# A two-layer mixer kernel: the layer change in two token halves, and the recurrence's short convolution one block ahead

## The chip, the core and the metric

The kernel runs on one core of a Trainium2 chip. The metric is the device time of one execution in microseconds (us). A core has a matrix engine (PE; its weight loads are listed apart as PEld), a vector engine (DVE), a scalar engine (ACT), GpSimd (POOL) and a queue that issues DMAs (SP). Each engine runs its own instructions in order; between engines there are only semaphores.

## What is computed

Two layers over 256 latent and 256 context tokens of width 2048, float32. A layer normalises and modulates its input, multiplies it with one wide matrix, runs three branches on the columns (a convolution module, a recurrence in both directions, attention), gates them, and multiplies with an output matrix:

```
def mixer_layer(x, xc, ...):
    h, gate = modulate(x, norm_g, (c_act @ w_ada + b_ada)[:, None, :])
    hc, gate_c = modulate(xc, norm_g, cc_act @ w_ada + b_ada)
    u = h @ w_in
    uc = hc @ (w_in[:, :OFF_MEM_END] if last else w_in)
    ...
    x = x + gate * (jnp.concatenate([y_conv, y_lru, y_attn], axis=-1) @ w_out)
    if not last:
        xc = xc + gate_c * (jnp.concatenate([yc_conv, yc_lru, yc_attn], axis=-1) @ w_out)

def modulate(x, norm_g, ada):                       # rmsnorm is x * rsqrt(mean(x*x) + EPS) * g
    shift, scale, gate = jnp.split(ada, 3, axis=-1)
    return rmsnorm(x, norm_g) * (1 + scale) + shift, gate

def rglru_scan(x, h0, conv_w, conv_b, w_r, b_r, w_i, b_i, lam):
    xc = depthwise_conv(x, conv_w, conv_b, (LRU_CONV_WIDTH - 1, 0))      # four taps
    r = sigmoid(blocks(xc) @ w_r + b_r);  i = sigmoid(blocks(xc) @ w_i + b_i)
    log_a = -LRU_C * r * softplus(-lam);  a = exp(log_a)
    bx = sqrt(-expm1(2 * log_a)) * (i * xc)
    # h[t] = a[t] * h[t-1] + bx[t], by an associative scan
```

## The kernel before

**Layout and blocks.** Activations lie transposed: the partition is the channel, the free axis the token (0 to 255 latent, 256 to 511 context). `Y` [128, 16, 512] holds the stream, and in layer 1 the context half of its rows is free for the branches. A layer is `NB` = 56 blocks of 128 output columns: 4 recurrence inputs `x`, keys and values `k`, `v`, the convolution's `b` and `a` (in layer 1 these eight come first: b4 is `b0`, b5 `a0`, up to b11 `a3`; then `k0`, `k1`, `v0`, `v1` as b12 to b15), queries, gates, and from `B_OUT` = 40 on 16 output blocks. In the text bN is block N of a layer.

**Products.** A float32 matrix is split in a high part, rounded by ACT (`hi`, L962), and a rest, from DVE (`lo`, L1261); activations too (`h_hi`, `h_lo`). A block is 16 tiles deep, three products each (hi by hi, hi by lo, lo by hi; L756 to L758), so 48 products, made in two halves of 24 (`mm_half`). There are four buffers of half a block of weights (a unit `u` uses `u % 4`), so `hi` of a unit waits for the products of the unit four before. A product has 512 columns where all tokens are needed, 256 in layer 1's latent-only blocks. Every engine's program walks over the same blocks; in block b ACT and DVE prepare the weights of block b + 2, then take the result of block b out of PSUM (`evac`), then do the side work that tables such as `LRU_TAPS`, `LRU_MM` and `CONV_TAPS` assign to the block.

**Layer change.** Output block b54 and b55 end layer 0. DVE adds each output block, times its gate, to the residual (L1398), ACT squares it (L991), DVE adds the squares up (L1306). PE sums over partitions with a matrix of ones (`rms_mm`, L670 and L672), ACT takes the root (L998), DVE the reciprocal (`rstd`, L1339). Then DVE modulates tile k (L1326), ACT rounds it (L1004), DVE makes the rest (L1333). In that time PE makes `gate_sum` (L623) and `bridge(4)`, 32 products whose result nobody reads (L631). Layer 1 opens with four blocks side by side in four PSUM banks: `mm_first_quarter` does tiles 0 to 3 for all four (48 products, L712 to L714), then `mm_quarter` the rest, two blocks at a time.

**Recurrence.** Four groups t of 128 channels, two directions d. `taps` (DVE, L1428 and L1432, 8 instructions) is the four-tap convolution, into `T[:, 4 * d]`; `lru_mm` (PE, L780) four float32 products that read it; `lru_act` (ACT, L1048 to L1063) two gates and their powers; `lru_v` (DVE, L1438, L1440); `lru_sqrt` (ACT); `lru_scan` (DVE, L1447 to L1461), which ends in the same `T[:, 0]` and `T[:, 4]`. So `taps` of group t + 1 must wait for the scan of group t. In the tables a list is for layer 0, one for layer 1, and the entries are the blocks of t = 0 to 3; within a block DVE runs `lru_v`, `lru_scan` and `taps` after the evacuation.

## Time and profile before

| | us |
|---|---|
| median of 3 runs (1279.43 to 1281.43) | 1280.09 |
| the profiled execution's own time | 1280.23 |
| span of its trace | 1278.4 |
| PE busy | 1229.1 |
| DVE busy | 794.5 |
| ACT busy | 542.5 |

The profiled execution lies 0.14 us from the median, and 1.83 us of its time are outside the span. Times in the text are us from the start of the span. Idle time of an engine counts only where the chain that ended last goes through it.

### The profile page before, as it was taken

How to read it: one execution, taken by the hardware profiler on the slowest of the kernel's cores; microseconds unless marked ns; L12 is line 12 of the kernel's file. 1: busy time of each engine (PE TensorE's matmuls, PEld its weight loads, DVE VectorE, ACT ScalarE, POOL GpSimd, SP SyncE). 2: the span in 40 equal slices, each digit the busy share in tenths (PEclk: the TensorE clock that was granted, in tenths of full speed). 3: DMA queues.
4: the chain of work that ended last, by engine and by line, in shares of the span. 5: the costliest groups of instructions: out<-in, count | busy, mean ns of one | idle time of the engine just before them, and what ended most of it. 6: DMA issues, size and time to landing. Idle time of an engine off the chain costs nothing.

```text
span 1278.4 us, 16662 instructions
## 1 busy us (share of the span) xinstructions
PE 1229.1 (96%) x6722; PEld 972.0 (76%) x6722; DVE 794.5 (62%) x1249; ACT 542.5 (42%) x853; POOL 9.8 (1%) x11
## 2 busy tenths in 40 slices
PE   3999999999999999999999999999999999999995
PEld 1555776667677777776778888788787988889995
DVE  5344446687566676663466555695689977646554
ACT  5222444452233434453342222354656455475442
POOL 0000100000000000000100000000000000000000
PEclk9999999999999999999999999999999999999998
DMA  9999755446663343332438666413332544325542
GB/s 334 350 348 348 233 211 202 198 198 259 251 246 147 139 176 132 132 132 99 177 137 280 222 222 222 173 66 132 132 104 70 200 144 151 122 87 197 189 165 66
DMA packets 80877, 236.34 MB, mean 185 GB/s; under 512 B 9376, under 2 KB 54176, under 8 KB 59424
## 3 DMA queue, kind: packets, MB, share of 16 engines
q1 hardware_dynamic: 80800, 235.27, 52.0%
q8 instruction: 53, 0.87, 0.3%
q14 instruction: 24, 0.20, 0.0%
HBM read 230.54 MB, written 2.10 MB: 182 GB/s over the span
## 4 chain that ended last, share of the span: by engine, by line
PE 88%; DVE 4%; ACT 3%; SPq 3%; issue 1%; DMA 1%; DVEq 0%; ACTq 0%
PE psum_block L756 21%; PE psum_block L757 21%; PE psum_block L758 21%; PE psum_ada L614 3%; PE psum_scores L780 2%; SPq L563 2%; PE psum_ada L651 2%; PE psum_scores L692 1%; PE psum_scores L817 1%; PE psum_scores L694 1%; PE psum_scores L693 1%; PE psum_scores L850 1%; PE psum_scores L830 1%; DVE T L1432 1%; PE psum_block L877 1%
## 5 line engine op out<-in xcount | busy, mean ns | idle before, releaser
L756 PE MATMUL psum_block<-h_hi,w_hi 128*128 128x512 f32 (+1 forms) x1616 | 556.0, 344 | 2.3 <-DVE h_lo L1253 1.7
L757 PE MATMUL psum_block<-h_lo,w_hi 128*128 128x512 f32 (+1 forms) x1616 | 547.7, 339 | 0.0
L758 PE MATMUL psum_block<-h_hi,w_lo 128*128 128x512 f32 (+1 forms) x1616 | 547.6, 339 | 0.0
L1261 DVE TENSOR_TENSOR w_lo<-raw,w_hi 128x1024 fp32r<-128x1024 f32 x210 | 254.3, 1223 | 312.2 <-ACT w_hi L962 312.0
L962 ACT ACTIVATE w_hi<-raw 128x1024 fp32r<-128x1024 f32 x210 | 221.1, 1058 | 486.6 <-PE psum_block L758 454.0
L756 PEld LDWEIGHTS psum_block<-h_hi,w_hi 128*128 128x128 f32 x1616 | 306.4, 190 | 65.3 <-issue 26.5
L757 PEld LDWEIGHTS psum_block<-h_lo,w_hi 128*128 128x128 f32 x1616 | 306.6, 190 | 33.8 <-issue 1.9
L758 PEld LDWEIGHTS psum_block<-h_hi,w_lo 128*128 128x128 f32 x1616 | 306.5, 190 | 33.8
L1474 DVE SCALAR_TENSOR_TENSOR Y<-glu,small,Y 128x512 f32<-128x512 f32 (+1 forms) x240 | 130.4, 611 | 0.0
L1077 ACT ACTIVATE T<-psum_scores,stats 128x512 f32<-128x512 f32 (+1 forms) x48 | 28.9, 616 | 46.5 <-DVE stats L1522 46.5
L614 PE MATMUL psum_ada<-raw,cstat 128*32 128x512 f32 x384 | 47.8, 600 | 0.0
L1004 ACT ACTIVATE h_hi<-T,ada 128x256 fp32r<-128x256 f32 x64 | 27.8, 499 | 43.2 <-DVE T L1326 43.2
L1261 DVE TENSOR_TENSOR w_lo<-qreg,w_hi 128x1024 fp32r<-128x1024 f32 (+1 forms) x16 | 17.5, 1092 | 30.3 <-ACT w_hi L962 29.2
L780 PE MATMUL psum_scores<-T,bd 128*128 128x512 f32 x64 | 30.8, 626 | 5.5 <-DVE T L1432 5.5
L1295 DVE SCALAR_TENSOR_TENSOR kv<-raw,cstat,kv 128x2048 f32<-128x2048 f32 x15 | 35.2, 2343 | 0.2
L1438 DVE SCALAR_TENSOR_TENSOR qreg<-qreg,T 128x512 f32<-128x512 f32 x16 | 10.3, 687 | 37.8 <-ACT qreg L1063 37.8
L1083 ACT ACTIVATE T<-T,stats 128x512 f32<-128x512 f32 (+1 forms) x48 | 27.3, 641 | 13.6 <-DVE stats L1532 13.6
L1432 DVE SCALAR_TENSOR_TENSOR T<-qreg,small,T 128x512 f32<-128x512 f32 x48 | 32.5, 745 | 0.0
L991 ACT ACTIVATE T<-Y 128x512 f32<-128x512 f32 (+1 forms) x48 | 25.7, 548 | 16.0 <-DVE Y L1398 13.3
L962 ACT ACTIVATE w_hi<-qreg 128x1024 fp32r<-128x1024 f32 (+1 forms) x16 | 15.1, 945 | 30.7 <-DMA qreg<-in_w_blocks 30.7
L1306 DVE TENSOR_TENSOR T<-T 128x512 f32<-128x512 f32 (+1 forms) x43 | 25.7, 599 | 3.2 <-ACT T L991 1.8
L692 PE MATMUL psum_scores<-h_hi,w_hi 128*128 128x512 f32 x64 | 27.7, 433 | 0.0
(200 smaller groups left out, 1183.5 us busy)
## 6 DMA issues: line engine op xcount, KB each, us to landing
raw<-in_w_blocks SPq DMA_DIRECT2D x105, 1024.0 KB, 4.9
raw<-in_w_ada SPq DMA_DIRECT2D x81, 1024.0 KB, 6.8
qreg<-in_w_blocks SPq DMA_DIRECT2D x8, 896.0 KB, 11.6
glu<-in_w_ada SPq DMA_DIRECT2D x5, 1024.0 KB, 11.9
...
```

The lines of the kernel that those rows point to most:

```text
L614: last = mm(psA[32 * j:32 * j + 32, :], cstat[:, c_at(k):c_at(k) + 32], w[:, j * TOK:(j + 1) * TOK], start=(k == 0), stop=(k == DT - 1), t ...
L692: mm(ps, hi, hh[:, k, :], start=(k == 0), stop=False)
L756: mm(ps[:, 0:n], hi, hh[:, k, t], start=(at == 0), stop=False)
L757: mm(ps[:, 0:n], hi, hl[:, k, t], start=False, stop=False)
L758: last = mm(ps[:, 0:n], lo, hh[:, k, t], start=False, stop=(at == DT - 1))
L780: last = mm(psS[:, 2 * d + g, :], bd[:, g, d * CT + t, :], T[:, 4 * d, :], start=True, stop=True)
L962: fn(wh[:, u % 4, 0:cols.stop - cols.start], raw_of(item)[:, cols], ACT.Copy).then_inc(*C.up("hi", u))
L1077: fn(T[:, g, k0:TOK], psS[:, g, k0:TOK], ACT.Exp, scale=SCALE, bias=st[:, 1, g:g + 1], accum_out=st[:, 2, g:g + 1]).then_inc(*C.up("att_ex ...
L1261: V.tensor_tensor(wl[:, u % 4, 0:n], raw_of(item)[:, cols], wh[:, u % 4, 0:n].bitcast(F32), ALU.subtract).then_inc(*C.up("lo", u))
L1295: stt(acc, w, cstat[:, c_at(k):c_at(k) + 1], acc, ALU.mult, ALU.add).then_inc(*C.up("gate_acc", k))
L1432: stt(out, x, lcw[:, c, k:k + 1], out, ALU.mult, ALU.add).then_inc(*C.up("taps", l, t, d))
L1474: stt(out, x, dwh[:, c:c + 1], out, ALU.mult, ALU.add).then_inc(*C.up("conv", l, t, k))
```

## The change

1. **Output blocks by token half.** Blocks b54 and b55 of layer 0 are made in the order: latent columns of b54, latent of b55, then context of b54, context of b55 (eight pieces of 24 products with 256 columns). The four weight buffers are held until the context pieces. `evac_half` takes each half out by itself.
2. **Two norm chains.** Squares, sum, root, reciprocal, modulation and rests are made by token half (`norm_in_halves` on ACT and DVE, `rms_mm_half` on PE). The sum over partitions of the latent half stands between the pieces of the context half; that of the context half after the first tile of the first quarter.
3. **First quarter in halves.** `mm_first_quarter` does tiles 0 to 3 with the latent columns, then with the context columns. `rms_mm(1)` and `bridge(4)` are gone, `gate_sum` stays.
4. **Recurrence.** `taps` writes to `lru_x(t, d)`, rows 8 to 15 of `Y` in the context columns, two sets in turn. It stands a block or two earlier for t = 1 to 3. `lru_mm` of layer 1 is at b6, b9, b11, b13 (it was b6, b9, b12, b14). `lru_v` goes with `lru_sqrt` (`LRU_ROOT`), the scan one block behind it, and both are now ahead of the second `lo` of a block on DVE. `lru_act(t)` waits for the scan of t - 1. Eight entries of layer 1's `CONV_TAPS` differ, with the same sum.

Line numbers in the rows of after are those of the changed kernel.

```diff
-BRIDGE = [14, 4, 6, 8, 32]
-
-
-LRU_TAPS = [[7, 9, 11, 13], [4, 7, 10, 13]]
-LRU_MM = [[8, 10, 12, 14], [6, 9, 12, 14]]
-LRU_SCAN = [[9, 11, 13, 15], [7, 10, 13, 15]]
+BRIDGE = [14, 4, 6, 8]
+SPLIT_FROM = NB - 2
+
+
+LRU_TAPS = [[7, 8, 10, 12], [4, 6, 9, 11]]
+LRU_MM = [[8, 10, 12, 14], [6, 9, 11, 13]]
+LRU_ROOT = [[9, 11, 13, 15], [7, 10, 12, 14]]
+LRU_SCAN = [[10, 12, 14, 16], [8, 11, 13, 15]]
 CONV_AT = [12, 8]
 CONV_TAPS = [[4, 3, 2, 3, 3, 4, 3, 3, 3, 3, 4, 3, 3, 3, 3, 3, 3, 3, 3, 3],
-             [3, 0, 2, 3, 3, 8, 6, 3, 1, 2, 3, 2, 1, 3, 2, 4, 4, 1, 2, 3, 3, 3]]
+             [1, 1, 2, 0, 6, 7, 6, 5, 1, 2, 3, 2, 1, 3, 2, 4, 4, 1, 2, 3, 3, 3]]
...
+        def lru_x(t, d):
+
+            m = 8 + 4 * (t % 2) + 2 * d
+            return Y[:, m:m + 2, LAT:TOK]
...
                     pe.wait_ge(*C.at("lo", quarter_unit(0, pair)))
                 for b in range(2):
                     pe.wait_ge(*released(NB + b - 2))
-                pe.wait_ge(*C.at("rms_std", 1))
-                for i in range(QT):
-                    pe.wait_ge(*C.at("h_lo", 1, i))
-                    for pair in range(SIDE // 2):
-                        quarter_products(0, pair, i)
+                for s in range(2):
+                    for i in range(QT):
+                        pe.wait_ge(*C.at("h_lo", 1, i, s))
+                        for pair in range(SIDE // 2):
+                            quarter_products(0, pair, i, tokens(s))
+                        if s == 0 and i == 0:
+                            rms_mm_half(1)
 
             def mm_quarter(quarter, pair):
 
                 pe.wait_ge(*C.at("lo", quarter_unit(quarter, pair)))
                 for i in range(QT):
                     if pair == 0:
...
                 for i in range(DT // 2):
                     at = j * DT // 2 + i
                     k = k_tile(b, at)
                     if b == B_OUT:
                         pe.wait_ge(*C.at("y_lo", l, k))
                     hi, lo = wh[:, slot, i * P:(i + 1) * P], wl[:, slot, i * P:(i + 1) * P]
-                    mm(ps[:, 0:n], hi, hh[:, k, t], start=(at == 0), stop=False)
-                    mm(ps[:, 0:n], hi, hl[:, k, t], start=False, stop=False)
-                    last = mm(ps[:, 0:n], lo, hh[:, k, t], start=False, stop=(at == DT - 1))
-                last.then_inc(*C.up("mm", u))
+                    mm(ps[:, cols], hi, hh[:, k, t], start=(at == 0), stop=False)
+                    mm(ps[:, cols], hi, hl[:, k, t], start=False, stop=False)
+                    last = mm(ps[:, cols], lo, hh[:, k, t], start=False, stop=(at == DT - 1))
+                if s != 0:
+                    last.then_inc(*C.up("mm", u))
+                elif j:
+                    last.then_inc(*C.up("mm_lat", gb))
 
             def misc_free(l):
...
@@ -901,9 +935,7 @@
                 if b == 0:
                     scores_free.clear()
                     if l:
-                        rms_mm(l)
                         gate_sum()
-                        bridge(4)
                         mm_first_quarter()
                         for quarter in range(1, 4):
                             for pair in range(SIDE // 2):
...
                         for g in range(GROUPS):
                             mm_group(g)
                 if b < OPEN[l]:
+                    continue
+                if in_halves(gb):
+                    mm_half(gb, 0, 0)
+                    mm_half(gb, 1, 0)
+                    if b == NB - 1:
+                        mm_half(gb - 1, 0, 1)
+                        rms_mm_half(0)
+                        mm_half(gb - 1, 1, 1)
+                        mm_half(gb, 0, 1)
+                        mm_half(gb, 1, 1)
                     continue
                 mm_half(gb, 0)
 
...
+            def norm_in_halves():
+
+
+                square_half(DT - 2, 0)
+                square_half(DT - 1, 0)
+                hi(quarter_unit(0, 0))
+                rms_std_half(0)
+                hi(quarter_unit(0, 1))
+                square_half(DT - 2, 1)
+                modulate_list([(k, 0) for k in range(QT)])
+                hi(quarter_unit(1, 0))
+                square_half(DT - 1, 1)
+                hi(quarter_unit(1, 1))
+                modulate_list([(QT, 0)])
+                rms_std_half(1)
+                modulate_list([(k, 1) for k in range(QT + 1)] + [(k, i) for k in range(QT + 1, 2 * QT) for i in range(2)])
 
             def evac(gb):
                 l, b = divmod(gb, NB)
...
@@ -1043,6 +1122,8 @@
             def lru_act(l, t):
 
                 act.wait_ge(*C.at("lru_mm", l, t))
+                if t:
+                    act.wait_ge(*C.at("lru_h", l, t - 1))
...
+                dve.wait_ge(*C.at("rms_add", 1, m - 1))
+                V.tensor_tensor(T[:, 4, w], T[:, 4, w], T[:, squares(1)[m % 2], w], ALU.add).then_inc(*C.up("rms_add", 1, m, s))
+
+            def rstd_half(s):
+                dve.wait_ge(*C.at("rms_std", 1, s))
+                V.reciprocal(tbuf[:, tokens(s)], tbuf[:, tokens(s)]).then_inc(*C.up("rstd", 1, s))
+                dve.wait_ge(*C.ago("rstd"))
+
+            def norm_in_halves():
+
+
+                rms_add_half(DT - 2, 0)
+                evac_half(NB - 1, 0)
+                lo(quarter_unit(0, 0))
+                rstd_half(0)
+                evac_half(NB - 2, 1)
+                h_list([(k, 0) for k in range(QT)])
+                lo(quarter_unit(0, 1))
+                rms_add_half(DT - 2, 1)
+                evac_half(NB - 1, 1)
+                lo(quarter_unit(1, 0))
+                h_list([(QT, 0)])
+                rstd_half(1)
+                h_list([(k, 1) for k in range(QT)])
+                lo(quarter_unit(1, 1))
+                h_list([(QT, 1)] + [(k, i) for k in range(QT + 1, 2 * QT) for i in range(2)])
 
             def rstd(l):
                 n = TOK if l < LAYERS else LAT
...
+            def evac_half(gb, s):
+
+                i, w = gb - B_OUT, tokens(s)
+                dve.wait_ge(*(C.at("mm", unit(0, gb, 1)) if s else C.at("mm_lat", gb)))
+                if s == 0:
+                    dve.wait_ge(*C.at(f"xs{i % 2}", i))
+                stt(Y[:, i, w], bank(gb)[:, w], ada[:, 0, s, GATE * DT + i:GATE * DT + i + 1], T[:, i % 2, w], ALU.mult, ALU.add
+                    ).then_inc(*(C.up("evac_dve", gb) if s else C.up("evac_lat", gb)))
 
             def evac(gb):
                 l, b = divmod(gb, NB)
...
                 dve.wait_ge(*C.at("evac_act", l * NB + t))
-                if t:
-                    dve.wait_ge(*C.ago("lru_h"))
+                if t > 1:
+                    dve.wait_ge(*C.at("lru_g", l, t - 2, 1))
                 for k in range(LTAPS):
                     for d in range(2):
                         c = (l * 2 + d) * CT + t
                         s = k if d == 0 else 2 * (LTAPS - 1) - k
                         x = lrux[:, t, :, s:s + LAT]
-                        out = segs(T[:, 4 * d, :])
+                        out = lru_x(t, d)
                         if k == 0:
                             V.tensor_scalar(out, x, lcw[:, c, 0:1], at["lcb"][:, c:c + 1], ALU.mult, ALU.add
...
                     continue
                 if b == B_OUT:
                     y_lo(l, b)
-                if gb + 2 < GLOB:
+                if gb == NB - 1:
+                    norm_in_halves()
+                    continue
+                if gb + 2 < GLOB and not in_halves(gb):
                     lo(unit(0, gb + 2, 0))
+                if b in LRU_ROOT[l]:
+                    lru_v(l, LRU_ROOT[l].index(b))
+                if b in LRU_SCAN[l]:
+                    lru_scan(l, LRU_SCAN[l].index(b))
                 if l == 0 and b == B_OUT - 1:
                     y_lo(l, b)
```

PE at the layer change, from the last output products to the first of layer 1. Before: the sum over partitions (`psum_scores<-T`), the gate's sum (`psum_ada<-kv`), the bridge (`psum_scores<-rounded`), then the first quarter:

```order
L758 MATMUL psum_block<-h_hi,w_lo 128x512
L670 MATMUL psum_scores<-T,small 128x512
L672 MATMUL psum_scores<-T,small 128x512
L623 MATMUL psum_ada<-kv,small 32x512 x4
L631 MATMUL psum_scores<-rounded 128x384 x32
L712 MATMUL psum_block<-h_hi,w_hi 128x512
```

After:

```order
L787 MATMUL psum_block<-h_hi,w_hi 128x256
L788 MATMUL psum_block<-h_lo,w_hi 128x256
L789 MATMUL psum_block<-h_hi,w_lo 128x256
L636 MATMUL psum_ada<-kv,small 32x512 x4
L735 MATMUL psum_block<-h_hi,w_hi 128x256
L736 MATMUL psum_block<-h_lo,w_hi 128x256
```

The gate's sum now stands directly between the last output product and the first of layer 1, and the latent half's sum over partitions stands 72 products ahead of it. The context half's sum is inside the first quarter.

DVE at the layer change. Before: last evacuation of b55 (L1398), last squares, rest of the fourth unit of weights, reciprocal, then the tiles of layer 1:

```order
L1398 SCALAR_TENSOR_TENSOR Y<-psum_block,ada,T 128x256 x2
L1306 TENSOR_TENSOR T<-T 128x512
L1261 TENSOR_TENSOR w_lo<-raw,w_hi 128x1024
L1339 RECIPROCAL tbuf<-tbuf 128x512
L1326 SCALAR_TENSOR_TENSOR T<-Y,A,tbuf 128x256 x4
```

After, from the latent evacuation of b55 to its context evacuation:

```order
L1496 SCALAR_TENSOR_TENSOR Y<-psum_block,ada,T 128x256
L1340 TENSOR_TENSOR w_lo<-raw,w_hi 128x1024
L1442 RECIPROCAL tbuf<-tbuf 128x256
L1496 SCALAR_TENSOR_TENSOR Y<-psum_block,ada,T 128x256
L1404 SCALAR_TENSOR_TENSOR T<-Y,A,tbuf 128x256 x2
L1410 SCALAR_TENSOR_TENSOR h_lo<-T,ada,h_hi 128x256
L1404 SCALAR_TENSOR_TENSOR T<-Y,A,tbuf 128x256
L1410 SCALAR_TENSOR_TENSOR h_lo<-T,ada,h_hi 128x256
L1404 SCALAR_TENSOR_TENSOR T<-Y,A,tbuf 128x256
L1410 SCALAR_TENSOR_TENSOR h_lo<-T,ada,h_hi 128x256 x2
L1340 TENSOR_TENSOR w_lo<-raw,w_hi 128x1024
L1438 TENSOR_TENSOR T<-T 128x256
```

The evacuation of b55's context half (the next L1496) is behind four latent tiles and a rest of weights.

DVE in layer 1, from b6 on. Before: rests for b8, then `lru_v(0)`, rests for b9, the scan of t = 0, `taps(1)`:

```order
L1261 TENSOR_TENSOR w_lo<-raw,w_hi 128x1024 x2
L1438 SCALAR_TENSOR_TENSOR qreg<-qreg,T 128x512 x2
L1440 SCALAR_TENSOR_TENSOR T<-T 128x512 x2
L1261 TENSOR_TENSOR w_lo<-raw,w_hi 128x1024 x2
L1374 SCALAR_TENSOR_TENSOR glu<-tbuf,psum_block 128x256
L1447 TENSOR_TENSOR T<-T,qreg 128x512 x2
L1451 SCALAR_TENSOR_TENSOR T<-T 128x256
L1454 SCALAR_TENSOR_TENSOR T<-T 128x512
L1457 SCALAR_TENSOR_TENSOR T<-T 128x256
L1461 TENSOR_TENSOR Y<-T 128x256
L1428 TENSOR_SCALAR T<-qreg,small 128x512 x2
L1432 SCALAR_TENSOR_TENSOR T<-qreg,small,T 128x512 x6
```

After (L1562 and L1566 are `taps`, L1572 and L1575 `lru_v`, L1582 the first of the scan):

```order
L1340 TENSOR_TENSOR w_lo<-raw,w_hi 128x1024 x2
L1562 TENSOR_SCALAR Y<-qreg,small 128x2x256 x2
L1566 SCALAR_TENSOR_TENSOR Y<-qreg,small,Y 128x2x256 x6
L1340 TENSOR_TENSOR w_lo<-raw,w_hi 128x1024
L1572 SCALAR_TENSOR_TENSOR qreg<-qreg,T 128x512 x2
L1575 SCALAR_TENSOR_TENSOR T<-T,Y 128x512 x2
L1340 TENSOR_TENSOR w_lo<-raw,w_hi 128x1024
L1508 SCALAR_TENSOR_TENSOR glu<-tbuf,psum_block 128x256
L1340 TENSOR_TENSOR w_lo<-raw,w_hi 128x1024
L1582 TENSOR_TENSOR T<-T,qreg 128x512 x2
```

`taps(1)` moved from behind the scan of t = 0 to ahead of `lru_v(0)`, and `lru_v` and the scan to between the two rests of a block.

## Rows read from the trace of the kernel before

**Rows 1.** The page: the chain that ended last, by engine.

```profile
PE 88%; DVE 4%; ACT 3%; SPq 3%; issue 1%; DMA 1%; DVEq 0%; ACTq 0%
```

**Rows 2.** PE's waits: waiting line, releaser: us in total, times, longest.

```profile
PE psum_scores L780 <- DVE T L1432: 5.5, 3, 2.8
```

**Rows 3.** PE in order of time, layer change: start, us, line, operation, count, [idle before].

```profile
798.57 0.39 PE L756 MATMUL psum_block<-h_hi,w_hi 128*128 128x512 f32 x1
...
820.11 0.39 PE L758 MATMUL psum_block<-h_hi,w_lo 128*128 128x512 f32 x1
822.06 1.13 PE L670 MATMUL psum_scores<-T,small 128*128 128x512 f32 x2 [1.57 <-DVE T L1306]
...
823.98 1.07 PE L623 MATMUL psum_ada<-kv,small 128*32 128x512 f32 x8
824.97 5.82 PE L631 MATMUL psum_scores<-rounded 128*128 128x384 f32 x32
831.05 0.47 PE L712 MATMUL psum_block<-h_hi,w_hi 128*128 128x512 f32 x1 [0.26 <-DVE h_lo L1333]
...
842.03 0.39 PE L712 MATMUL psum_block<-h_hi,w_hi 128*128 128x512 f32 x1
```

**Rows 4.** PE in order of time, b5 of layer 1.

```profile
883.74 0.28 PE L756 MATMUL psum_block<-h_hi,w_hi 128*128 128x256 f32 x1
883.86 0.28 PE L757 MATMUL psum_block<-h_lo,w_hi 128*128 128x256 f32 x1
```

**Rows 5.** PE in order of time, final norm: a sum over partitions with 256 columns.

```profile
1265.11 0.70 PE L670 MATMUL psum_scores<-T,small 128*128 128x256 f32 x2 [0.91 <-DVE T L1306]
1265.65 0.59 PE L672 MATMUL psum_scores<-T,small 128*128 128x256 f32 x2
```

**Rows 6.** ACT in order of time, layer change.

```profile
809.71 1.06 ACT L962 ACTIVATE w_hi<-raw 128x1024 fp32r<-128x1024 f32 x1 [4.38 <-PE psum_block L758]
...
823.04 1.28 ACT L998 ACT_TABLE_LOAD   x1
```

**Rows 7.** DVE in order of time: layer change, then a reciprocal of the final norm.

```profile
812.73 2.34 DVE L1295 SCALAR_TENSOR_TENSOR kv<-raw,cstat,kv 128x2048 f32<-128x2048 f32 x1
...
830.94 0.88 DVE L1326 SCALAR_TENSOR_TENSOR T<-Y,A,tbuf 128x256 f32<-128x256 f32 x2
...
832.65 0.88 DVE L1326 SCALAR_TENSOR_TENSOR T<-Y,A,tbuf 128x256 f32<-128x256 f32 x2
...
1267.39 1.75 DVE L1339 RECIPROCAL tbuf<-tbuf 128x256 f32<-128x256 f32 x1 [2.33 <-ACT tbuf L998]
```

**Rows 8.** Groups of DVE instructions from 760 to 880: count | busy, mean ns.

```profile
L1261 DVE TENSOR_TENSOR w_lo<-raw,w_hi 128x1024 fp32r<-128x1024 f32 x21 | 25.7, 1225 | 39.8 <-ACT w_hi L962 39.6
```

**Rows 9.** SP's queue in order of time, layer change.

```profile
801.18 0.33 SPq L563 DMA_DIRECT2D raw<-in_w_ada  x1
...
804.65 0.50 SPq L504 DMA_DIRECT2D T<-in_xT  x1
```

**Rows 10.** DMAs of line L563, 790 to 850: from issue to landing.

```profile
DMA to landing us min/median/max: 4.6/4.9/6.1
```

**Rows 11.** PE in order of time: four of the recurrence's eight product groups.

```profile
208.83 3.70 PE L780 MATMUL psum_scores<-T,bd 128*128 128x512 f32 x8 [0.66 <-DVE T L1432]
...
916.05 5.40 PE L780 MATMUL psum_scores<-T,bd 128*128 128x512 f32 x8 [2.80 <-DVE T L1432]
...
943.70 3.60 PE L780 MATMUL psum_scores<-T,bd 128*128 128x512 f32 x8
...
971.08 3.70 PE L780 MATMUL psum_scores<-T,bd 128*128 128x512 f32 x8 [2.00 <-DVE T L1432]
```

**Rows 12.** DVE in order of time, layer 1: scan of t = 0, then `taps(1)`.

```profile
906.81 1.28 DVE L1447 TENSOR_TENSOR T<-T,qreg 128x512 f32<-128x512 f32 x2
...
911.93 4.06 DVE L1432 SCALAR_TENSOR_TENSOR T<-qreg,small,T 128x512 f32<-128x512 f32 x6
```

**Rows 13.** Stretches: us, busy time and count of each engine, granted clock, DMA.

```profile
900.00:920.00 20.00, 17.20 (x117) 14.68 (x116) 18.07 (x28) 12.40 (x15) 0.00 (x0) 0.91 0.18 58
```

135 lines of the change are left out of this document (89 added, 46 removed).

## The prediction

> **What bounds the kernel.** I read the page's chain first: PE holds 88% of it [rows 1], so only time in which PE stands still, or makes something that the result doesn't need, can be won. PE's waits come next: after the start of the program the largest is that of the recurrence's products, 5.5 us in three pieces [rows 2]. Then PE in order of time. At the layer change the last output product starts at 820.11. PE stands still 1.57 us until the squares are summed, makes the sum over partitions (822.06 to 823.98, that is 1.92), the gate's sum (0.99) and then the bridge (824.97 to 831.05, 6.08 with the wait behind it), whose result nobody reads [rows 3]. It covers the chain root, reciprocal, modulation. In all 10.7 us lie between the end of layer 0's products (820.34) and the first of layer 1 (831.05), and 2.9 of them are needed work. The rest of the change touches the recurrence: of eight groups of products, five show no idle time before them and three do, 0.66, 2.80 and 2.00 us, each released by the last of `taps` [rows 11].
>
> **Part 1: output blocks in halves.** 96 products with 512 columns become 192 with 256. The two blocks now take 798.57 to 820.34, 226.8 ns a product [rows 3]. Layer 1's products with 256 columns start 120 ns apart [rows 4]. A pair costs 13.2 ns more than a whole; 96 pairs make 1.27 us, the first quarter's 48 make 0.63. The cost is 1.9 us, all of it on PE's path. The same weights, operands and banks are behind both rows, so I take it as it is.
>
> The row shows 120 ns for 256 columns and 227 for 512. The Trainium skill, page "TensorE: Matmul & The Clock Gate", section "Back-to-back issue gap", gives N / 2.4 + 2.5 ns at the full clock, that is 109 and 216: by it a pair costs 2.5 ns more, 0.4 us in all, and the sum below would be 1.5 us lower. The rows differ from it and they decide.
>
> **Part 2: PE's new calendar at the change.** Eight pieces of 24 products take 2.88 us each. From 798.57: latent half of b54 ready at 804.3, of b55 at 810.1; first context piece of b54 to 812.97; the latent sum over partitions, by the final norm's two lines 0.54 + some 0.43, so 0.97 [rows 5]; second piece of b54 to 816.8, b55 to 819.7 and 822.6; the gate's sum 0.99 to 823.6. From there on PE could begin layer 1.
>
> Is the latent sum ready? `evac_half` of b54 at 804.8, the gate's accumulation 2.34 [rows 7], whose weights are issued at 801.18 and land 4.9 later, at 806.1 [rows 9, 10], squares and adds by 809.3. The residual of b55, issued at 804.65 [rows 9], takes about as long and lands at 809.6, ahead of 810.1. `evac_half` of b55, then the square, are done at 811.1: 1.9 us early. The two moved DMAs have no later start than before, since SP waits for the accumulation of gate rows 14, which doesn't move.
>
> **Part 3: the chain on DVE and ACT.** ACT rounds unit 1 of layer 1 when the first context piece is done (0.25 after it, as the row at 809.71 stands to its product), 813.2 to 814.3, loads the root's table (1.28) [rows 6], and makes the root of 256 columns by 816.1, since the sum is there at 814.2. DVE: rest of the unit (1.23) [rows 8] to 815.5; reciprocal of 256 columns 1.75 [rows 7] to 817.85; context evacuation of b54 to 818.3. A tile with both halves takes DVE 830.94 to 832.65, 1.71 [rows 7], so a half tile 0.86; four latent half tiles with 0.3 to fill the pipe end at 822.05. Behind them on DVE are the rest of unit 2 (to 823.25), an add of squares (0.4) and the context evacuation of b55 (0.45), at 824.1. `mm_first_quarter` waits for both, the unit and `released`, which is this evacuation; queued behind it on PE is all of layer 1. So **layer 1 starts at 824.15**, 0.55 us after PE is free.
>
> Latent part of the quarter: 48 products, 5.76, with the context sum (0.97) after the first 12, which ends at 826.6. To 830.9. The context chain from 826.6: root 0.45 (the table is loaded), reciprocal 1.75 to 829.05, two modulations, first rest at 830.3, then 0.86 for each further tile. PE wants them at 830.9, 832.3, 833.8 and 835.2: no wait, with 0.6 us in hand at the first. Context part to 836.65. The second quarter wants tiles 4 to 7 at 836.65 and then every 1.36. DVE makes a rest of weights to 833.8 and seven half tiles at 0.86, to 840.1, and PE wants the last at 840.7. Later quarters have over 1 us in hand. Before, the second quarter began at 842.03 [rows 3]. **Won: 842.03 − 836.65 = 5.4 us**, the 1.9 of part 1 already in it. The bridge's and the first idle time's 7.7 go, 1.9 come, 0.55 are the new wait; the rest is rounding.
>
> **Part 4: recurrence.** The three waits for `taps` are 0.66 (layer 0) and 2.80 + 2.00 (layer 1). Behind the one of 2.80 the group took 5.40 us against 3.60 for one without [rows 11], and the granted clock of 900 to 920 is 0.91 [rows 13]: after that idle time a part of the work ran at 1.2 GHz instead of 2.4. Together 0.66 + 2.80 + 2.00 + 1.80 = 7.3 us.
>
> Do the waits go? From 906.81 to 915.99 DVE makes the scan and then `taps(1)` [rows 12], while PE stands still from 913.25. After, `taps(1)` follows the rests for b8, is done by 900 in the old calendar and is wanted at 913.25. `taps(2)` is wanted at 913.25 + 3.5 + 11.5 = 928.3. DVE's work from 904.5 (first rest for b9) to its end: `lru_v` 2.4, five rests 6.0, two evacuations 0.8, scan 4.1, convolution 0.7, taps 5.0, 19.0 us, so 923.5. `taps(3)` is wanted 25 us later still, with 16 us of work ahead of it. The second rest of each block now stands behind `lru_v` or a scan: that of b10 is done at 915.1 and wanted at 919.6, that of b11 at 918.2 and wanted at 925.3. ACT's group t waits for the scan of t − 1: for t = 2 this is at 936.3 instead of 931.7, and the first unit behind it on ACT, for b14, is wanted 14 us after. In layer 0 blocks take twice as long and all of this has more in hand. `taps` has the same instructions, now written in two segments of 256, and `lru_mm` reads them so. No row shows that. The six of L1432 already read two segments and take 4.06 [rows 12]; I take 0 for both, with half a us either way in the range.
>
> **Sum.** 5.4 + 7.3 = 12.7 us. The profiled execution took 1280.23; less 12.7 is 1267.5. It stands 0.14 above the median, so against the median of 1280.09 I say **1267.4**. Not on a changed path are the start of the program and everything from b17 of layer 1 on, which moves as a whole.
>
> **Rivals.**
> A, the new queue on DVE decides at the layer change. The context evacuation of b55 stands behind ten instructions and four handoffs to ACT, and the context chain has only 0.6 in hand. If each handoff costs 0.3 more, the start slips by 1.2 and the context tiles by as much; two us are lost, and with an idle time near the 2.80 that cost clock in [rows 11, 13] another 1.8. For it: DVE's busy time from 813 on is without a gap in my calendar. Against it: the half tile's 0.86 has the handoffs of two halves in it. Time 1267.4 + 2 to 3.8 = 1269.4 to 1271.2.
> B, the recurrence doesn't deliver: its waits come back as waits for rests of weights in b10 to b12, because `lru_v` and the scan (6.5 us) now stand ahead of them. It begins when DVE is more than 4.5 us behind my calendar at b10. Then half of the 7.3 is lost: 1271.0.
> C, slower than before: without the bridge the clock falls. PE makes 0.97 of small work and has 0.55 idle at 823, and if that brought the granted clock to its lower level, products would take twice as long. To eat 12.7 us it has to last for more than 12.7 us of PE's work, from the change to past the middle of the second quarter; over both quarters (22.9 us of work) it is + 22.9, so 1290. Against it: 1.57 idle at 820 is followed by no slow product, and the dip behind 2.80 idle cost 1.8 only [rows 3, 11].
> The same page of the Trainium skill, section "What's actually happening", says that the clock's default is the lower level and activity lifts it, which would put C's start where the array has little to do; the trace agrees with that direction at 916, and not at 822.
> D, the change doesn't do what it says at one place, as when the half sums wait for each other: PE waits in the first quarter for the context chain by several us, and 5.4 becomes 2. 1270.8.
>
> **Chances.** Forecast 0.68, A 0.16, B 0.06, D 0.05, C 0.03, more gain than forecast 0.02. The forecast's own range: without the new wait it is 0.55 lower, and the slower first products behind each idle time may save 0.8 more; the calendar's rounding may cost 1.4. So from 1266.0 to 1268.8. A, B and D reach to 1271.2. The range for 8 in 10 goes from 1265.8 to 1271.0. A measurement of this kernel tells 0.2% (2.6 us) from no change; all but C and a stray case lie below 1277.5: faster 0.95, same 0.02, slower 0.03.
>
> **What would show it.** Right: the idle time before the first quarter in PE's order of time is under 1 us; the second quarter starts 5.4 us earlier than 842.03; the only idle time of PE in the quarters is there; no wait of the recurrence's products for `taps`; each of the eight groups 3.6 to 3.7 us long; the stretch of 20 us about b9 at a granted clock of 1.00. Wrong: a wait of PE for the evacuation or a rest at the change over 1.5 us (A), waits for the rests of weights about b10 (B), a granted clock under 1 from 823 on (C), waits for `h_lo` inside the quarters (D). Products of 256 columns more than 120 ns apart would move part 1.

## The result, and the profile of the changed kernel

| | before | after |
|---|---|---|
| median of 4 runs, us | 1280.76 (1279.43 to 1281.45) | 1269.27 (1268.70 to 1270.52) |
| the profiled execution | 1280.23 | 1269.71 |
| span of its trace | 1278.4 | 1267.9 |

The ratio is 0.9904, with a 95% interval from 0.9887 to 0.9922. The changed kernel is 11.5 us faster by the medians and 10.5 by the profiled executions. I had said 1267.4 (12.7 us won), in a range of 1265.8 to 1271.0.

To see where the time went, I set the start of the same product in both traces side by side, at the places where one stage gives way to the next:

| first product of | before | after | gained since the row above |
|---|---|---|---|
| b7 of layer 0 | 153.89 | 155.07 | −1.19 |
| b54 of layer 0 | 798.57 | 798.97 | +0.80 |
| b4 of layer 1 | 874.67 | 869.95 | +5.12 |
| b9 of layer 1 | 907.33 | 903.79 | −1.20 |
| b10 of layer 1 | 920.88 | 912.64 | +4.71 |
| b17 of layer 1 | 992.07 | 981.54 | +2.29 |
| last product | 1263.92 | 1253.40 | 0.00 |

Each gain is the difference of the two columns, less what the rows above it had already gained. Two rows are negative, and neither was in my sum. The rest adds up to 12.9, against 12.7 in the sum.

PE's waits in the trace of after (columns: waiting group, what released it, us in total, times, longest):

```profile
PE psum_scores L680 <- DVE T L1385: 20.0, 1, 20.0
...
PE psum_block L787 <- DVE glu L1508: 1.0, 1, 1.0
...
PE psum_block L735 <- DVE Y L1496: 0.9, 1, 0.9
```

The entry that was second to the opening's in [rows 2], 5.5 us for `taps`, is gone: no wait of the recurrence's products (now L814) is left. Two are new. L735 is the first quarter's product, held by the context evacuation of b55 (L1496). L787 is a product of b9, held by an evacuation (L1508).

The layer change on PE in order of time, trace of after (start, duration, form, count, and the idle time ahead with its releaser):

```profile
813.36 0.59 PE L692 MATMUL psum_scores<-T,small 128*128 128x256 f32 x2
...
822.72 0.28 PE L789 MATMUL psum_block<-h_hi,w_lo 128*128 128x256 f32 x1
822.93 1.06 PE L636 MATMUL psum_ada<-kv,small 128*32 128x512 f32 x8
824.85 0.36 PE L735 MATMUL psum_block<-h_hi,w_hi 128*128 128x256 f32 x1 [0.85 <-DVE Y L1496]
...
837.28 0.40 PE L735 MATMUL psum_block<-h_hi,w_hi 128*128 128x512 f32 x1
```

Against [rows 3]: 2.0 us instead of 10.7 lie between the end of layer 0's products (822.84, one spacing of 0.12 behind the start of the last) and layer 1's first (824.85). The latent sum (813.36) runs without a wait between the context pieces, and the second quarter starts at 837.28 instead of 842.03.

The same place on DVE, trace of after, with the context evacuation of b55 at 824.12 and what stands ahead of it:

```profile
816.50 1.75 DVE L1442 RECIPROCAL tbuf<-tbuf 128x256 f32<-128x256 f32 x1 [0.56 <-ACT tbuf L1047]
818.29 0.48 DVE L1496 SCALAR_TENSOR_TENSOR Y<-psum_block,ada,T 128x256 f32<-128x256 f32 x1
...
822.65 1.22 DVE L1340 TENSOR_TENSOR w_lo<-raw,w_hi 128x1024 fp32r<-128x1024 f32 x1
823.78 0.42 DVE L1438 TENSOR_TENSOR T<-T 128x256 f32<-128x256 f32 x1
824.12 0.48 DVE L1496 SCALAR_TENSOR_TENSOR Y<-psum_block,ada,T 128x256 f32<-128x256 f32 x1
...
830.78 0.49 DVE L1410 SCALAR_TENSOR_TENSOR h_lo<-T,ada,h_hi 128x256 fp32r<-128x256 f32 x1 [0.18 <-ACT h_hi L1055]
```

The new loss stands ahead of b9. On PE, and on DVE in the 6 us before it, trace of after:

```profile
902.48 0.28 PE L789 MATMUL psum_block<-h_hi,w_lo 128*128 128x256 f32 x1
903.79 0.36 PE L787 MATMUL psum_block<-h_hi,w_hi 128*128 128x256 f32 x1 [1.04 <-DVE glu L1508]
```
```profile
898.55 1.23 DVE L1340 TENSOR_TENSOR w_lo<-raw,w_hi 128x1024 fp32r<-128x1024 f32 x1 [3.43 <-ACT w_hi L1004]
899.69 1.28 DVE L1572 SCALAR_TENSOR_TENSOR qreg<-qreg,T 128x512 f32<-128x512 f32 x2
900.89 1.29 DVE L1575 SCALAR_TENSOR_TENSOR T<-T,Y 128x512 f32<-128x512 f32 x2
902.10 1.22 DVE L1340 TENSOR_TENSOR w_lo<-raw,w_hi 128x1024 fp32r<-128x1024 f32 x1
903.23 0.41 DVE L1508 SCALAR_TENSOR_TENSOR glu<-tbuf,psum_block 128x256 f32<-128x256 f32 x1
```

PE could begin b9 at 902.6, but its PSUM bank is that of b7, and b7's result is taken out at 903.23. Two rests of weights and the four instructions of `lru_v` (L1572, L1575) are queued ahead of that. Ahead of the first rest DVE stood idle for 3.43 us.

The recurrence's products (shortest, median and longest in ns), and two stretches with their granted clock (PEclk), trace of after:

```profile
L814 PE MATMUL psum_scores<-Y,bd x64: 590/592/595, 179.8 to 952.8; 128*128 128x512 f32 x64
```
```profile
core 0: us, PE busy (x) PEld busy (x) DVE busy (x) ACT busy (x) POOL busy (x), PEclk, DMA share, GB/s
820.00:835.00 15.00, 14.14 (x116) 13.03 (x114) 12.95 (x23) 6.38 (x12) 0.00 (x0) 1.00 0.40 141
892.00:912.00 20.00, 18.96 (x144) 17.54 (x143) 16.30 (x24) 15.59 (x20) 0.00 (x0) 1.00 0.29 103
```

Not one of the 64 products lasts over 595 ns, and the clock is at its upper level about the change and about b9, where [rows 13] had 0.91.

### The profile page after: what moved, and what is told of

Its sections match the earlier page's. It is cut to its first block, busy times and chain, and to the rows that moved or that the text cites. A ratio compares the mean times of both kernels' runs of the same rounds, so it can differ in the third digit from the quotient of the medians.

```text
span 1267.9 us, 16907 instructions
## 1 busy us (share of the span) xinstructions
PE 1223.3 (96%) x6838; PEld 975.4 (77%) x6838; DVE 796.6 (63%) x1251; ACT 544.3 (43%) x856; POOL 9.7 (1%) x11
## 4 chain that ended last, share of the span: by engine, by line
PE 91%; ACT 3%; DVE 2%; SPq 2%; DMA 1%; issue 1%; DVEq 0%; ACTq 0%
PE psum_block L787 22%; PE psum_block L788 21%; PE psum_block L789 21%; PE psum_ada L627 4%; PE psum_ada L664 2%; PE psum_scores L814 2%; PE psum_scores L715 1%; SPq L576 1%; PE psum_scores L717 1%; PE psum_scores L716 1%; PE psum_scores L851 1%; PE psum_scores L884 1%; PE psum_scores L864 1%; DMA bd<-in_w_ada 1%; PE psum_block L911 1%; PE psum_misc L911 1%
## 5 line engine op out<-in xcount | busy, mean ns | idle before, releaser
L787 PE MATMUL psum_block<-h_hi,w_hi 128*128 128x256 f32 (+1 forms) x1648 | 561.9, 341 | 3.4 <-DVE h_lo L1332 1.7
L788 PE MATMUL psum_block<-h_lo,w_hi 128*128 128x256 f32 (+1 forms) x1648 | 553.4, 336 | 0.0
L789 PE MATMUL psum_block<-h_hi,w_lo 128*128 128x256 f32 (+1 forms) x1648 | 553.2, 336 | 0.0
L787 PEld LDWEIGHTS psum_block<-h_hi,w_hi 128*128 128x128 f32 x1648 | 312.6, 190 | 65.2 <-issue 28.2
L788 PEld LDWEIGHTS psum_block<-h_lo,w_hi 128*128 128x128 f32 x1648 | 312.9, 190 | 32.8 <-issue 1.9
L789 PEld LDWEIGHTS psum_block<-h_hi,w_lo 128*128 128x128 f32 x1648 | 312.8, 190 | 32.7
L1566 DVE SCALAR_TENSOR_TENSOR Y<-qreg,small,Y 128x512 f32<-128x512 f32 x48 | 32.5, 748 | 0.0
L1033 ACT ACTIVATE T<-Y 128x512 f32<-128x512 f32 (+1 forms) x46 | 24.5, 546 | 12.9 <-DVE Y L1532 10.1
L1410 DVE SCALAR_TENSOR_TENSOR h_lo<-T,ada,h_hi 128x256 fp32r<-128x256 f32 x64 | 27.9, 481 | 1.7 <-ACT h_hi L1055 1.7
L814 PE MATMUL psum_scores<-Y,bd 128*128 128x512 f32 x64 | 28.8, 592 | 0.0
L1404 DVE SCALAR_TENSOR_TENSOR T<-Y,A,tbuf 128x256 f32<-128x256 f32 x64 | 27.7, 481 | 0.6
## 6 DMA issues: line engine op xcount, KB each, us to landing
qreg<-in_w_blocks SPq DMA_DIRECT2D x8, 896.0 KB, 11.7
```

The source lines that it names most:

```text
L787: mm(ps[:, cols], hi, hh[:, k, t], start=(at == 0), stop=False)
L788: mm(ps[:, cols], hi, hl[:, k, t], start=False, stop=False)
L789: last = mm(ps[:, cols], lo, hh[:, k, t], start=False, stop=(at == DT - 1))
L814: last = mm(psS[:, 2 * d + g, :], bd[:, g, d * CT + t, :], lru_x(t, d), start=True, stop=True)
L1566: stt(out, x, lcw[:, c, k:k + 1], out, ALU.mult, ALU.add).then_inc(*C.up("taps", l, t, d))
```

## The experiments

Each experiment was timed in several runs beside the kernel before on the same chip; kernels timed together share those runs. Two traces are compared from the first product of b7 of layer 0 on where the openings differ.

### The same program again, and the two parts alone

**after_again** is the changed kernel once more. 

> The changed kernel once more, unchanged, beside the kernels that take it apart. Two theories of the 1.2 us that it had lost by b7 of layer 0, where it has the same instructions as before: by the first it is the spread of the opening's DMAs, and the first product of b7 starts anywhere from 153.9 (before) to 155.1 (after) in each kernel, whatever it holds; by the second it belongs to the changed program, and b7 starts at 155.1 here too and in each kernel that has the halves. All else as in the trace of after: second quarter about 4.9 us earlier than before counted from b7, a wait of 1.0 us of PE ahead of b9 of layer 1. Ratio to before 0.989 to 0.992.

Measured: 1269.43 us (1268.25 to 1270.45) against 1281.72 (1278.42 to 1284.22), ratio 0.9898 [0.9885, 0.9912]. In its trace b7 starts at 153.89, exactly as before, and from there every place of the table above is 1.2 us earlier than in the first trace of after. The instructions are the same. What differs lies ahead of 60 us: the lengths of the waits for the first DMAs, and the granted clock, which from 36 to 44 is 0.57 in the first trace of after, 0.79 here and 1.00 in before. So the row −1.19 is not the change's. Against this trace the span of before is 11.73 us longer.

**halves_only** keeps parts 1 to 3 and takes part 4 back:

```diff
-LRU_TAPS = [[7, 8, 10, 12], [4, 6, 9, 11]]
-LRU_MM = [[8, 10, 12, 14], [6, 9, 11, 13]]
-LRU_ROOT = [[9, 11, 13, 15], [7, 10, 12, 14]]
-LRU_SCAN = [[10, 12, 14, 16], [8, 11, 13, 15]]
+LRU_TAPS = [[7, 9, 11, 13], [4, 7, 10, 13]]
+LRU_MM = [[8, 10, 12, 14], [6, 9, 12, 14]]
+LRU_SCAN = [[9, 11, 13, 15], [7, 10, 13, 15]]
+LRU_ROOT = LRU_SCAN
...
-            m = 8 + 4 * (t % 2) + 2 * d
-            return Y[:, m:m + 2, LAT:TOK]
+            return segs(T[:, 4 * d, :])
```

> The layer change in halves with the recurrence as it was. Additive theory: it gains at the layer change what the traces of before and after show there, 5.1 us (5.4 forecast), nothing elsewhere: the three waits for the taps are back (0.7, 2.8, 2.0) with the slow group behind the one of 2.8, and there is no wait ahead of b9. Time 1275.4 for a before of 1280.5, ratio 0.996. Rival, that the layer change's gain is lost when DVE comes out of it with less in hand: PE waits more for taps in layer 1, gain 3 us or less.

Measured: 1277.38 us, ratio 0.9958 [0.9946, 0.9970], span 1273.4, 5.09 less than before. The waits for `taps` are back, and with them the group at the lower clock:

```profile
PE psum_scores L813 <- DVE T L1563: 5.5, 3, 2.8
```
```profile
911.01 1.22 PE L813 MATMUL psum_scores<-T,bd 128*128 128x512 f32 x1 [2.81 <-DVE T L1563]
```

Its b9 starts 5.76 us after b8 (896.52, 902.28), that is without the new wait.

**recurrence_only** is before with part 4 alone, the same lines in the other direction. 

> The recurrence's edits with the layer change as it was. Additive theory: 0.8 us in layer 0 and 5.8 in layer 1, in which the new wait of 1.2 ahead of b9 (for the evacuation of a1, b7, now behind lru_v on DVE) is already taken off: 6.6 us, time 1273.9, ratio 0.995; this wait stands here too. Rival: the wait ahead of b9 comes from the earlier layer change, with DVE still behind from it; then it isn't here, and the gain is 7.8 us, ratio 0.994.

Measured: 1273.67 us, ratio 0.9936 [0.9924, 0.9948], span 1271.8, 6.64 less than before. The wait ahead of b9 is in it, of the same size:

```profile
PE psum_block L762 <- DVE glu L1382: 1.0, 1, 1.0
```

5.09 and 6.64 make 11.73, the whole of `after_again`. The medians confirm the sum, and split it otherwise: against the 1281.72 of before in these runs 4.34 and 8.05 are won, 12.39 together, and 12.29 by `after_again`. The traced execution of `halves_only` (1275.14) is the fastest of its five, and the 17 of before go from 1278.42 to 1284.22, so each share is known no better than to a microsecond or so. The parts don't touch each other, and the new wait belongs to part 4. The layer change doesn't cause it.

### Where `lru_v` and the scan stand

**side_work_behind** is the changed kernel with `lru_v` and the scan back behind the evacuation, in their new blocks (the four lines stood ahead of the block's second `lo`, and now follow `evac`):

```diff
-                if b in LRU_ROOT[l]:
-                    lru_v(l, LRU_ROOT[l].index(b))
-                if b in LRU_SCAN[l]:
-                    lru_scan(l, LRU_SCAN[l].index(b))
...
+                if b in LRU_ROOT[l]:
+                    lru_v(l, LRU_ROOT[l].index(b))
+                if b in LRU_SCAN[l]:
+                    lru_scan(l, LRU_SCAN[l].index(b))
```

> The changed kernel with lru_v and the scan back behind the evacuation on DVE; taps stay early and in their own buffers. If the gain in the recurrence comes from taps alone, ahead and in two buffers, all of it stays (no wait of a recurrence product for taps), and the wait ahead of b9 goes: 1.2 us faster than the changed kernel. Rival, that lru_v and the scan had to be earlier: ACT's next group then waits for the scan, its rounding of weights comes late, and PE waits for w_lo or evacuations about b10 to b14: slower than the changed kernel by 1 us or more.

Measured: 1282.74 us (11 runs), ratio 1.0008 [0.9998, 1.0019], span 1280.8, which is 14.1 over `after_again`. The wait ahead of b9 is gone (905.74 to 911.50, 5.76 us), so that much of the theory holds, and far more is lost elsewhere. In layer 0 alone it is 9.6 us, nearly all of it in two places. At the first, ACT and then PE in the trace of `side_work_behind`:

```profile
274.30 0.69 ACT L1129 ACTIVATE T<-psum_scores,small 128x512 f32<-128x512 f32 x1 [3.73 <-DVE Y L1596]
```
```profile
281.10 0.66 PE L650 MATMUL psum_ada<-rounded,lnr 128*128 128x128 f32 x4 [2.60 <-ACT lnr L1014]
```

`lru_act` waits for the scan of the group before (part 4 put this wait in), 3.73 us here and none for the scan in `after_again`. ACT's copy out of `psum_ada` (L1014) is queued behind `lru_act`, and PE waits 2.60 us for it. At the second place, DVE, ACT, SP's queue and PE:

```profile
304.17 1.29 DVE L1582 TENSOR_TENSOR T<-T,qreg 128x512 f32<-128x512 f32 x2
```
```profile
308.64 0.60 ACT L1114 ACTIVATE qreg<-psum_block 128x512 f32<-128x512 f32 x1 [5.64 <-DVE Y L1596]
```
```profile
309.26 2.41 SPq L537 DMA_DIRECT2D lnr<-qreg  x4
311.72 1.05 SPq L576 DMA_DIRECT2D raw<-in_w_ada  x2
```
```profile
316.91 1.06 PE L627 MATMUL psum_ada<-raw,cstat 128*32 128x512 f32 x8 [2.07 <-DMA raw<-in_w_ada]
```

ACT's evacuation of a query block writes to `qreg`, which the last scan still reads. DVE begins that scan at 304.17, and ACT stands for 5.64 us. The DMAs that copy from `qreg` (L537) go out when ACT is done, and those of the modulation weights (L576) stand behind them in SP's queue; PE waits 2.07 us for the first of the two and 1.43 for the second. Behind each place the products ran at the lower clock for over 3 us (0.59 from 281 to 285), a loss of some 1.8 each time. In layer 1 the same evacuation waits 3.68 us, the roundings of weights behind it are late, and PE waits 3.70 for a rest, with 1.4 of clock behind it. The 9.6 of layer 0, less 1.2 for the wait ahead of b9 and with some 5.3 here, are the 13.7 by which the last product is late, counted from b7. The rival has the first link, ACT's next group that waits for the scan, and puts the loss at b10 to b14 of layer 1. The larger part came in layer 0, by waits that it doesn't name.

**taps_only** tells the place from the block. It has `taps` early with its own buffers, `lru_v` behind the evacuation in the block of its products, the scan a block behind; the lines put in follow `evac`:

```diff
-LRU_SCAN = [[10, 12, 14, 16], [8, 11, 13, 15]]
+LRU_SCAN = [[9, 11, 13, 15], [7, 10, 12, 14]]
...
+                if b in LRU_MM[l]:
+                    lru_v(l, LRU_MM[l].index(b))
```

> The changed kernel with lru_v and the scan exactly where they were before: behind the evacuation, lru_v in the block of its products and the scan one block on. Taps stay early and in their own buffers. In side_work_behind they were a block later as well, and the query block's evacuation (ACT, L1114) waited for the last scan, 5.6 us in layer 0 and 3.7 in layer 1. Theory: there the block was the fault, not the place within it, and what the recurrence gains is due to taps: no wait for that scan here, b54 of layer 0 within 0.2 us of the changed kernel's counted from b7, no wait ahead of b9, and 1.2 us under the changed kernel. Rival: DVE, which waits for ACT's gates in lru_v at the end of the block (6.8 us before), comes late with the rests of weights of layer 1's short blocks now that products follow each other faster: PE waits for w_lo about b9 to b12, 1 us or more over the changed kernel.

Measured: 1277.78 us, ratio 0.9966 [0.9954, 0.9979], span 1276.0, 9.3 over `after_again`. Layer 0 agrees with `after_again` to 0.0 us, counted from b7, so it was the later block that cost 9.6 there. The theory's gain of 1.2 doesn't come all the same: layer 1 loses at b9, b10 and b12, and its rival had the place right, with another waiter, the evacuation and `taps` instead of the rests. DVE, then PE, about b9:

```profile
895.99 1.29 DVE L1572 SCALAR_TENSOR_TENSOR qreg<-qreg,T 128x512 f32<-128x512 f32 x2 [6.84 <-ACT qreg L1144]
...
899.31 4.06 DVE L1566 SCALAR_TENSOR_TENSOR Y<-qreg,small,Y 128x512 f32<-128x512 f32 x6
903.29 2.35 DVE L1340 TENSOR_TENSOR w_lo<-raw,w_hi 128x1024 fp32r<-128x1024 f32 x2
905.56 0.42 DVE L1508 SCALAR_TENSOR_TENSOR glu<-tbuf,psum_block 128x256 f32<-128x256 f32 x1
```
```profile
906.12 0.56 PE L787 MATMUL psum_block<-h_hi,w_hi 128*128 128x256 f32 x1 [4.44 <-DVE glu L1508]
930.82 5.40 PE L814 MATMUL psum_scores<-Y,bd 128*128 128x512 f32 x8 [1.80 <-DVE Y L1566]
```

DVE stands idle for 6.84 us until ACT's gates are there, then `lru_v(0)` and `taps(1)` run in a row with the rests and the evacuation of b7 behind them, and PE waits 4.44. Behind that the granted clock of 906 to 911 is 0.54, and 2.0 us more are gone by b10. The wait of 1.80 for `taps(2)` and the slow group behind it are the loss at b12. In the changed kernel `lru_v` comes a block later, behind a rest, when its operands have long been there. So early taps with buffers of their own are not enough: at 1277.8 this kernel is no better than `halves_only`, which has none of part 4 (1277.4). Moving `lru_v` and the scan away from the gates that they wait for is what lets DVE make `taps` and the evacuation in time.

### The two new waits

**evac_first** takes b7's result out ahead of that block's rests and `lru_v`:

```diff
+                first = gb == NB + 7
+                if first:
+                    evac(gb)
...
-                else:
+                elif not first:
```

> The changed kernel with one evacuation moved: in b7 of layer 1 DVE takes a1 out ahead of the rests of weights and of lru_v, at a time when it waits for ACT. Theory: PE's wait ahead of b9 (1.0 us, 1.2 with the slower first products) is for this evacuation alone, so b9 starts 1.2 us earlier counted from b8 and the gain lasts: 1.2 us under the changed kernel in the same call's scale, ratio to before 0.989. Rival: the next thing is late there as well (the second rest for b9, done just ahead of the evacuation, or b8's tanh), and PE waits for that instead: 0.5 us or less.

Measured: 1267.30 us (1266.60 to 1269.51) against 1282.11, ratio 0.9888 [0.9870, 0.9906], span 1266.2. DVE and PE ahead of b9:

```profile
896.62 0.42 DVE L1508 SCALAR_TENSOR_TENSOR glu<-tbuf,psum_block 128x256 f32<-128x256 f32 x1 [1.93 <-PE psum_block L789]
898.12 1.22 DVE L1340 TENSOR_TENSOR w_lo<-raw,w_hi 128x1024 fp32r<-128x1024 f32 x1 [1.08 <-ACT w_hi L1004]
```
```profile
902.06 0.28 PE L789 MATMUL psum_block<-h_hi,w_lo 128*128 128x256 f32 x1
902.18 0.28 PE L787 MATMUL psum_block<-h_hi,w_hi 128*128 128x256 f32 x1
```

b8 to b9 takes 5.76 us instead of 6.95, and the 1.2 stay to the end, as expected. The evacuation sits in idle time of DVE. The cause of the row −1.20 is shown.

**evac55_early** puts the context evacuation of b55 ahead of the context add of b54 and of the fourth latent tile of the first quarter's four (ACT's rounding of that tile moves too and is not shown):

```diff
-                h_list([(k, 0) for k in range(QT)])
+                h_list([(k, 0) for k in range(QT - 1)])
                 lo(quarter_unit(0, 1))
+                evac_half(NB - 1, 1)
                 rms_add_half(DT - 2, 1)
-                evac_half(NB - 1, 1)
+                h_list([(QT - 1, 0)])
```

> The changed kernel with DVE's order at the layer change altered: the fourth latent tile goes behind the context evacuation of b55 (and ACT's rounding of it behind the last square). Theory: PE's 0.85 ahead of the first quarter is DVE's queue in front of this evacuation, a half tile of it is 0.9, so PE starts when it is free: 0.9 us earlier. Rival: the context norm chain, with 0.6 in hand by the forecast, is then late, since the first context sum is earlier but DVE has the tile and a rest of weights ahead of the reciprocal: PE waits in the middle of the quarter, gain 0.3 or less.

Measured: 1269.68 us, ratio 0.9906 [0.9888, 0.9923]. The first quarter starts at 825.25 without a wait, 0.92 us earlier counted from b54. Then a wait stands in its middle; PE, and DVE ahead of it:

```profile
832.54 0.39 PE L735 MATMUL psum_block<-h_hi,w_hi 128*128 128x256 f32 x1 [0.43 <-DVE h_lo L1411]
```
```profile
826.55 1.22 DVE L1341 TENSOR_TENSOR w_lo<-raw,w_hi 128x1024 fp32r<-128x1024 f32 x1
827.69 0.48 DVE L1405 SCALAR_TENSOR_TENSOR T<-Y,A,tbuf 128x256 f32<-128x256 f32 x1
828.75 0.48 DVE L1411 SCALAR_TENSOR_TENSOR h_lo<-T,ada,h_hi 128x256 fp32r<-128x256 f32 x1 [0.58 <-ACT h_hi L1055]
829.15 1.75 DVE L1443 RECIPROCAL tbuf<-tbuf 128x256 f32<-128x256 f32 x1
```

PE takes the context tiles earlier than they come, because the reciprocal now stands behind a rest of weights and a further tile. Of 0.92 us 0.21 are left at b4, as the rival had it. The context chain has little slack, as the prediction's 0.6 us said, and a quarter that starts 0.9 earlier uses it up.

**both_mended** has both edits. 

> Both of these edits in one kernel. They lie 80 us apart, so if each holds, the sum holds: 2.1 us under the changed kernel, ratio to before 0.988. If only one is seen in it, the other was given back later.

Measured: 1266.93 us (1266.84 to 1268.05), ratio 0.9884 [0.9867, 0.9902], span 1266.2. Counted from b7, its last product starts 1.44 us earlier than in `after_again` (1251.72 − 154.87 = 1096.85 against 1252.18 − 153.89 = 1098.29). That is not the 2.1 expected but the 1.2 of `evac_first` with the 0.2 that `evac55_early` kept. It is the best of all kernels here and beats before clearly. That it beats the changed kernel rests on the two traces: the intervals of the two ratios to before overlap.

### The bridge and the clock

**no_bridge** is the kernel before without the 32 products of the bridge:

```diff
                         gate_sum()
-                        bridge(4)
                         mm_first_quarter()
```

> The kernel before, with the 32 products of bridge(4) left out and nothing else changed. PE then stands idle from the end of the gate's sum (824.97 in the trace of before) to the first quarter (831.05), 6.1 us. Theory 1 (what the idle time of 2.80 us at 913 showed holds here too): the clock of the first products behind it is at its lower level for some us; behind 2.80 us of idle time the loss was 1.8 us, so here 1.8 to 4 us, to be seen as first products further apart behind 831 and as a time of 1 to 4 us over the kernel before. The bridge then had its use in the kernel before, and the changed kernel can do without only because it has no idle time of over 1 us there. Theory 2 (rival C of the prediction, its strong form): the clock stays at its lower level through both quarters, 10 to 23 us over the kernel before. Theory 3: the bridge covered nothing, same time as before within 0.5 us, since the chain root, reciprocal, modulation sets the start of the first quarter.

Measured: 1282.38 us (1279.84 to 1287.59) against 1282.07, ratio 1.0006 [0.9991, 1.0021]. PE behind the gap, and the granted clock of 831 to 835, trace of `no_bridge`:

```profile
831.34 0.77 PE L712 MATMUL psum_block<-h_hi,w_hi 128*128 128x512 f32 x1 [6.01 <-DVE h_lo L1332]
831.91 0.63 PE L713 MATMUL psum_block<-h_lo,w_hi 128*128 128x512 f32 x1
...
835.53 0.40 PE L713 MATMUL psum_scores<-h_lo,w_hi 128*128 128x512 f32 x1
```
```profile
831.00:835.00 4.00, 3.66 (x9) 2.92 (x10) 3.93 (x11) 2.17 (x5) 0.00 (x0) 0.50 0.00 0
```

The start doesn't move (831.34, with an opening 0.3 later), and the first nine products stand 0.43 us apart instead of 0.23, at 1.2 GHz. The second quarter is 1.86 us later than before, counted from the first. Theory 1 holds at the place, not in the median, and theory 2, the strong form of rival C, is refuted: the lower level lasts some 4 us. On the Trainium skill, page "TensorE: Matmul & The Clock Gate", section "What's actually happening", the lower level is the default and activity lifts it; this trace agrees in direction.

The loss of 1.86 is not seen in the median, 0.3 above before with an interval up to +2.7. In the trace it is there to the end: counted from b7 the last product starts at 1111.87, in before at 1110.04. What the rows of two later groups of the recurrence's products show is how the clock differs between executions:

```profile
918.21 3.70 PE L780 MATMUL psum_scores<-T,bd 128*128 128x512 f32 x8 [2.82 <-DVE T L1431]
...
971.55 5.40 PE L780 MATMUL psum_scores<-T,bd 128*128 128x512 f32 x8 [2.00 <-DVE T L1431]
```

In [rows 11] it is the other way round: 5.40 behind 2.80 us of idle time, no loss behind 2.00. The two cancel here. But the 13 executions of before in these runs go from 1279.62 to 1284.36, the ten of `no_bridge` from 1279.84 to 1287.59, and in such a spread 1.8 us can't be told. What the bridge was worth in the kernel before is shown in one trace and open in the medians.

**bridge_back** is the changed kernel with `bridge(4)` behind `gate_sum()`. 

> The changed kernel with the 32 products of bridge(4) put back behind the gate's sum. Theory: they lie on the matrix engine's path now. The gate's sum ends at about 823.9 and the first quarter starts at 824.85 in the trace of the changed kernel; with the bridge's 5 to 6 us in between it starts at 829 to 830, so the kernel is 4 to 5 us slower than the changed kernel, about 1273 to 1274.5, and half of the gain of the layer change is gone. Nothing comes back from the clock, as it is at its upper level there without the bridge. Rival: the clock is lower behind the change in some executions of the changed kernel, or the first quarter has hidden waits for modulated tiles that the later start takes away; then less than 3.5 us are lost.

Measured: 1273.00 us (1272.49 to 1273.87), ratio 0.9932 [0.9918, 0.9947], span 1271.3. PE in its trace:

```profile
821.63 1.07 PE L636 MATMUL psum_ada<-kv,small 128*32 128x512 f32 x8
822.63 5.84 PE L644 MATMUL psum_scores<-rounded 128*128 128x384 f32 x32
828.31 0.28 PE L735 MATMUL psum_block<-h_hi,w_hi 128*128 128x256 f32 x1
```

The first quarter starts at 828.31 instead of 823.64 in `after_again`, and 4.59 us of it are still there at b4, 4.57 in the span. As expected: in the changed kernel the bridge covers little more than the wait of 0.85, and without it the clock is not lower.

## Why the prediction was right, and where not

**Part 1, the cost of the halves.** Right. The 192 half products of b54 and b55 start 120 ns apart, except for the latent sum between them: from 798.97 to 822.72 are 23.75 us, of which the sum takes some 0.9. The 109 ns by the formula for an isolated product (the Trainium skill, page "TensorE: Matmul & The Clock Gate", section "Back-to-back issue gap") don't hold for these products, neither in [rows 4] nor here. By that formula my gain would have been 1.5 larger (14.2), not lower as my sentence reads.

**Part 2, the calendar at the change.** Forecast 5.4, measured 5.12. In this trace b54 starts 0.40 later than in before, whose scale the prediction uses, so 0.40 has to come off its times. The binding wait is the one named, `released` by the context evacuation of b55: 0.85 instead of 0.55. The evacuation itself is within 0.1 us of my calendar (824.12 to 824.60, less 0.40, against 823.65 to 824.1). From its end to PE's first product (824.85) are 0.25 us, where I had 0.05, and this handoff is most of the 0.3. The residual and the latent sum were in time. Rival A has the same mechanism at a size of 2 us or more, and it did not come: the ten instructions and the handoffs between DVE and ACT keep the calendar within 0.3 us.

**Part 3, the chain.** Right nearly row by row, again with 0.40 to come off: the reciprocal at 816.50 to 818.25 (forecast to 817.85), the four latent tiles done at 822.7 (822.05), the first context rest from 830.78 to 831.27 (830.3), wanted by the context part at 831.5 (830.9). So it has 0.25 us in hand instead of 0.6, and there is no wait inside a quarter. D is out. `evac55_early` shows how thin this is: its quarter begins 0.9 us earlier and waits for the same rest.

**Part 4, the recurrence.** Its three waits and the slow group are gone: 0.80 + 4.71 + 2.29 = 7.8 against 7.3. The step that failed is DVE's calendar before b9. I summed all of DVE's work from 904.5 on and set it against `taps(2)`, at 928.3, and the rests of b10 and b11 against their products. I did not set the evacuation of b7 against the start of b9, which takes the same PSUM bank. My own numbers had it: from 904.5 a rest, `lru_v`, the second rest and the evacuation (1.2 + 2.4 + 1.2 + 0.4) end at 909.7, and b9 of before starts at 907.33. That is a wait of 2.4; the trace has 1.04, since the first rest starts 1.2 earlier than I had it (898.55, which is 903.3 counted as before does from b8). The wait, and not its size, could have been read. Rival B named the right queue and the wrong waiter.

**The sum.** 12.7 forecast. In the recorded trace 5.12 + 7.8 − 1.20 − 1.19 = 10.5; with the opening of `after_again`, 11.7, and with the medians 11.5. So one us was missed by the evacuation, 0.3 at the change, and half a us came back in the recurrence. The two losses that the sum lacked, the evacuation's and the opening's, are 1.2 each; the second is chance, and `after_again` doesn't have it.

**Rival C.** Not met, and its size was wrong as well: in `no_bridge` 6.01 us of idle time cost 1.86, about what 2.80 had. The term of 1.80 for the clock behind the wait at b10 was taken as sure. It is there in before and in `halves_only`, and in `no_bridge` not at that place but at another. The changed kernel ends both waits, so either way it wins it.
